# A two-layer hybrid decoder step on one core: all low weight halves of the first projection on GpSimd, four pairs of past rows to a weight block, small copies on ScalarE

## The reference, cut to what matters

```python
def even_project(x, w_in):
    h = jnp.einsum('btd,de->bte', x, w_in)
    a_val, a_glu, a_gate, q, kv_c, kv_s, kv_w, g, b_gate = jnp.split(h, offsets, axis=-1)
    u = a_val * jax.nn.sigmoid(a_glu)
    ...

def conv_branch(u_ext, a_gate, conv_w, conv_b, ln_g, ln_b):
    y = lax.conv_general_dilated(u_ext, conv_w[:, None, :], (1,), 'VALID', ...,
                                 feature_group_count=W_CONV) + conv_b
    return jax.nn.silu(layer_norm(y, ln_g, ln_b)) * jax.nn.silu(a_gate)

def compress_kv(kv, w_cmp):                # kv: 2048 past rows of a sequence, 256 wide
    ch = kv[:, :n_ch * CMP_STRIDE].reshape(B, n_ch, CMP_STRIDE, 2, KV_HEADS, HEAD_DIM)
    kc = (jnp.einsum('bnjchd,jchd->bnchd', ch[:, :-1], w_cmp[:CMP_STRIDE])
          + jnp.einsum('bnjchd,jchd->bnchd', ch[:, 1:], w_cmp[CMP_STRIDE:]))
```

## Time and profile before

| | us |
|---|---|
| median of 3 runs | 1334.58 (1334.31 to 1342.15) |
| the profiled execution, device time | 1331.57 |
| its span, first to last instruction | 1329.7 |
| PE busy | 1182.9 (89%) |
| DVE busy | 732.0 (55%) |
| POOL busy | 392.4 (30%) |
| ACT busy | 376.1 (28%) |

### The profile page before, as it was taken

How to read it: one execution, slowest core, us unless ns; L and a number is a source line. 1 busy time by engine, 2 the same in 40 slices (tenths; PEclk the granted TensorE clock), 3 DMA queues, 4 the chain that set the end, 5 groups by cost and what they waited for, 6 DMA issues and landing times.

```text
span 1329.7 us, 17791 instructions
## 1 busy us (share of the span) xinstructions
PE 1182.9 (89%) x7119; PEld 953.6 (72%) x7119; DVE 732.0 (55%) x1394; ACT 376.1 (28%) x791; POOL 392.4 (30%) x352
## 2 busy tenths in 40 slices
PE   5998999979989488899988999799969999978996
PEld 5998999979967244454544545478769999977883
DVE  2566889999934576445454454543435650065332
ACT  2211111111134454544545444511101121143000
POOL 3422200000012653432433323354412222124444
PEclk9998999989989588899999999899979999988998
DMA  7534333112130700040120301432112111041221
GB/s 225 184 108 154 112 96 80 32 32 48 32 157 0 263 11 1 1 159 1 45 114 1 159 1 69 129 106 93 52 52 79 47 47 39 9 145 52 95 95 40
DMA packets 77912, 105.22 MB, mean 79 GB/s; under 512 B 21280, under 2 KB 63912, under 8 KB 76607
## 3 DMA queue, kind: packets, MB, share of 16 engines
q1 hardware_dynamic: 69743, 69.62, 16.8%
q0 software_dynamic: 6016, 33.56, 6.8%
q10 hardware_dynamic: 2080, 1.05, 0.3%
HBM read 91.47 MB, written 17.69 MB: 82 GB/s over the span
## 4 chain that ended last, share of the span: by engine, by line
PE 63%; DVE 23%; ACT 5%; issue 4%; DMA 2%; POOL 1%; SPq 1%; POOLq 0%; ACTq 0%; DVEq 0%
PE PS L1511 15%; PE PS L1648 14%; DVE Y L543 9%; PE PS L648 9%; PE PS L1069 6%; PE PS L950 5%; PE PS L1083 3%; PE PS L640 2%; DVE ACC L495 2%; PE PS L1044 2%; PE PS L1003 2%; DVE WL L272 1%; PE PS L998 1%; ACT PRW L1109 1%; DVE PS L1163 1%
## 5 line engine op out<-in xcount | busy, mean ns | idle before, releaser
L648 PE MATMUL PS<-XH,WH 128*128 128x352 f32 (+1 forms) x648 | 149.2, 335 | 14.4 <-DVE WL L272 10.9
L543 DVE SCALAR_TENSOR_TENSOR Y<-U,SM,Y 128x1024 f32<-128x1024 f32 x120 | 145.9, 1279 | 0.2
L648 PE MATMUL PS<-XL,WH 128*128 128x352 f32 (+1 forms) x648 | 144.2, 327 | 0.0
L648 PE MATMUL PS<-XH,WL 128*128 128x352 f32 (+1 forms) x648 | 144.2, 327 | 0.0
L648 PEld LDWEIGHTS PS<-XH,WH 128*128 128x128 f32 (+1 forms) x648 | 110.0, 190 | 18.1 <-DVE WL L272 12.1
L648 PEld LDWEIGHTS PS<-XL,WH 128*128 128x128 f32 (+1 forms) x648 | 111.3, 189 | 1.4
L648 PEld LDWEIGHTS PS<-XH,WL 128*128 128x128 f32 (+1 forms) x648 | 111.0, 189 | 1.4
L1511 PE MATMUL PS<-WOH,XH 128*128 128x512 f32 (+1 forms) x288 | 94.2, 409 | 13.7 <-POOL WOL L1482 7.3
L495 DVE SCALAR_TENSOR_TENSOR ACC<-PS,SM,ACC 128x508 f32<-128x508 f32 x124 | 84.0, 740 | 40.5 <-PE PS L640 39.1
L950 PE MATMUL PS<-PT,TM 128*64 128x256 f32 x528 | 91.0, 425 | 12.4 <-ACT PT L1100 7.7
L1069 PE MATMUL PS<-KV,Q 64*128 64x512 f32 (+3 forms) x384 | 88.1, 515 | 15.2 <-ACT PRS L1109 12.4
(11 more groups left out here) (289 smaller groups left out, 2122.6 us busy)
## 6 DMA issues: line engine op xcount, KB each, us to landing
WRAW<-in_w_in_even SPq DMA_DIRECT2D x16, 512.0 KB, 4.3
WRAW<-in_w_in_odd SPq DMA_DIRECT2D x16, 512.0 KB, 3.9
XIN<-in_x_prompt SPq DMA_DIRECT2D x8, 512.0 KB, 12.5
WRAW<-in_w_in_even SPq DMA_DIRECT2D x16, 256.0 KB, 3.5
TM<-in_state_win_kv SPq DMA_DIRECT2D x8, 512.0 KB, 7.8
XR<-in_x_prompt SPq DMA_DIRECT2D x8, 512.0 KB, 3.5
layer_out<-R SPq DMA_DIRECT2D x8, 512.0 KB, 2.6
XR<-layer_out SPq DMA_DIRECT2D x8, 512.0 KB, 3.2
```

Source lines behind the costliest of these rows:

```text
L543: ins = v.scalar_tensor_tensor(dst, src, CWT[:, i, t:t + 1], dst, ALU.mult, ALU.add)
L648: ins = pe.matmul(PS[0:mcols, 3 * slot + c, 0:CH], w[:, slot, kk, 0:mcols], x[:, kk, c * CH:(c + 1) * CH], start=(kk == 0 and n == 0), sto ...
```

## The change

GpSimd makes all low halves, 0 to 26. Its program is now: low half m, then (for m below 8) gather m. Four pairs of past rows go with each of blocks 1 to 8, at `kk` = 0, 2, 4, 6. VectorE no longer makes low halves. Its order is: for each of blocks 1 to 8 four pairs, with `glu` behind the first pair of the even ones, and from block 5 on two taps or one behind the fourth pair; then 18 taps, `compress_prompt`, 6 taps, `conv_samples`, and the 94 taps that are left, in one go. The three small copies move to ScalarE, behind the evacuations of blocks 18 and 21.

```diff
-LOW_DVE = (6, 25)
 NPAIR = 32
+PER_BLOCK = 4
@@ pool_program @@
             low(po, 0)
             po.wait_ge(s_xt, 12)
             gather(0)
-            low(po, 1)
-            gather(1)
-            low(po, 2)
-            gather(2)
-            low(po, 3)
-            gather(3)
-            low(po, 4)
-            gather(4)
-            low(po, 5)
-            for n in range(5, 8):
-                gather(n)
-            for m in range(LOW_DVE[1], NM + 1):
-                po.wait_ge(s_wl, m)
+            for m in range(1, NM + 1):
                 low(po, m)
+                if m < 8:
+                    gather(m)
@@ act_program @@
                 evac(m)
                 if m + 2 <= NM:
                     high(m + 2)
+                if m == 18:
+                    act.wait_ge(s_ut, 1)
+                    act.activation(UROW[0:CW - 1, 0, :], PS[0:CW - 1, 6, :], ACT.Copy).then_inc(s_ue, 1)
+                    act.activation(UROW[:, 1, :], PS[0:NSAMP, 7, :], ACT.Copy).then_inc(s_ue, 1)
+                if m == 21:
+                    act.wait_ge(s_vct, 1)
+                    act.activation(VC[0:NCP, :], PS[0:NCP, 6, 0:P], ACT.Copy).then_inc(s_vc, 1)
@@ dve_program @@
-            def low_next(m):
-                if LOW_DVE[0] <= m < LOW_DVE[1]:
-                    v.wait_ge(s_wl, m)
-                    low(v, m)
-
-
-            for m in range(LOW_DVE[1]):
-                if m in (2, 4, 6, 8):
-                    glu(m // 2 - 1)
-                mine = range(min(3 * m - 3, NPAIR), min(3 * m, NPAIR)) if m else range(0)
-                few = 0 if m < 5 else (1 if m in (6, 8) else 2)
-                for n, p in enumerate(mine):
-                    compress(p)
-                    if m >= 5 and n < 2:
-                        taps(few if n else 1)
-                    if n == 1:
-                        low_next(m + 1)
-                if m and not mine:
-                    taps(3)
-                    low_next(m + 1)
-                    if m == 14:
-                        compress_prompt()
-                    elif m == 15:
-                        conv_samples()
-                        taps(3)
-                    else:
-                        taps(7)
-                if m == 19:
-                    v.wait_ge(s_ut, 1)
-                    v.tensor_copy(UROW[0:CW - 1, 0, :], PS[0:CW - 1, 6, :]).then_inc(s_ue, 1)
-                    v.tensor_copy(UROW[:, 1, :], PS[0:NSAMP, 7, :]).then_inc(s_ue, 1)
-                if m == 21:
-                    v.wait_ge(s_vct, 1)
-                    v.tensor_copy(VC[0:NCP, :], PS[0:NCP, 6, 0:P]).then_inc(s_vc, 1)
+
+            for m in range(1, 9):
+                for n in range(PER_BLOCK):
+                    compress(PER_BLOCK * (m - 1) + n)
+                    if n == 0 and m % 2 == 0:
+                        glu(m // 2 - 1)
+                if m >= 5:
+                    taps(2 if m % 2 else 1)
+            taps(18)
+            compress_prompt()
+            taps(6)
+            conv_samples()
             taps(len(TAPS))
@@ pe_program, one(m) @@
                 for kk in range(KT):
-                    if kk % 3 == 0 and 3 * (m - 1) + kk // 3 < NPAIR:
-                        compress(3 * (m - 1) + kk // 3)
+                    if kk % 2 == 0 and PER_BLOCK * (m - 1) + kk // 2 < NPAIR:
+                        compress(PER_BLOCK * (m - 1) + kk // 2)
                     ins = block(m, kk)
                 ins.then_inc(s_mm, 1)
```

## The result

| | before | after |
|---|---|---|
| median | 1334.44 us (4 runs, 1329.34 to 1342.15) | 1371.89 us (4 runs, 1360.68 to 1381.93) |
| ratio | | 1.025, 95% interval 1.016 to 1.033 |
| profiled execution, its span | 1331.57, 1329.7 | 1371.25, 1369.5 |
| end of block 8 | 166.3 | 172.4 |
| first mean | 371.1 | 403.5 |

The account below looks back on a forecast made before the run. TensorE, kept waiting by low halves that VectorE's taps lock out, bounds the first stage: 172.6 + 280.3 + 0.2 puts the first mean at 453.1, 82 us later. On 1331.6 that is 1413.6, plus 3.0 for the median: 1417, range 1330 to 1430.

Parts of the forecast that it names:

- the part with the pairs: Blocks 1 to 8, four pairs each: block 8 ends at 172.6 us, where it ended at 166.3.
- The turn of 3.93 us: From one pair's transposes to the next in blocks 1 to 8: 3.93 us, VectorE's, against 3.8 for TensorE alone.
- what glu and taps add: In blocks 1 to 8, VectorE's glu and taps between pairs make later pairs late, together 5 us.
- what is left without the collision: Rival "no cost": low halves run beside taps, TensorE bounds the first stage at 346.6, 24.3 less, 1310 us; chance 0.10.
- what a turn costs: Rival "a turn each": low halves enter at the next tap's end, VectorE pays 2.2 to 2.4; 1334 to 1338; chance 0.24.
- from one case to the other: The range: 1330, just below "a turn each" (0.24), to 1430, the upper end of "locked out" (0.58).
- I go by the earlier trace: Step taking a low half of 4.87 us, kept out until its taps ended, as the rule: "locked out", chance 0.58.
- three long waits: TensorE stands for low halves 10, 15 and 16, kept out by runs of taps: 14, 22 and 61 us.
- the two terms behind it: VectorE idle 9.6 us before `compress_prompt`, waiting for the store; lower TensorE clock after the long waits, 9 us.
- the two groups of rows: Earlier profile: a low half kept out by taps (4.87 us); a GpSimd subtraction let in between two VectorE ones (3.44).
- now and then: Rival: GpSimd wins some boundaries among the taps, so TensorE stands less; 1340 to 1410 us; chance 0.08.
- the yardstick: Start of the first mean, 371.1 before, forecast 453.1; its 82 us shift was carried to the kernel's end.

## Why the prediction was right and wrong

**Right: the part with the pairs.** Block 8 ended at 172.38, worked out as 172.6 (130.1 behind the first transposes, worked out as 130.9). The turn of 3.93 us held, and so did what glu and taps add.

**Right: what is left without the collision.** With a GpSimd that only writes the first mean starts at 345.7, worked out as 346.8; with the low halves on VectorE the sum for 354 was met at 354.8.

**Right: that GpSimd and VectorE exclude each other, and what a turn costs.** I had 2.2 to 2.4 us for a tap that gives way; measured 3.42 - 1.28 = 2.14. That the change came out slower is no luck either: the wait of 54.5 is one of the long waits forecast. That the time lies between 1330 and 1430 says little, since that range spans from one case to the other.

**Wrong: the step "I go by the earlier trace rows".** I took one low half that lost two boundaries for the rule, and made a sum of three long waits out of it: 14, 22 and 61 us for blocks 10, 15 and 16. Measured was one wait of 54.5, for block 20, and over three traces 7 losses in 23. The seven did what I had said of all (they waited until the run broke, the taps beside them at 1.20), but two thirds got in at once, as in the earlier trace rows. And a loser matters by where it falls: that of 197.50 lost two boundaries and cost TensorE nothing, since it was done in 5.12 and the slack was 7; early in the last run of 60 taps it costs what is left of the run. With it went the two terms behind it: low half 11 was never late, so the store of `ACC` didn't hold up `compress_prompt` (the 9.6 us of idleness; it began at 199.15, right behind the taps), and the lower clock was paid once (2.9 us), not three times. A sum with both behaviours, say some of the low halves losing and the last run of taps as the costly place, was what the two groups of rows allowed; I had it as a case of 0.08, "now and then", and gave it 1340 to 1410. The change lies in it.

**Too coarse: the yardstick.** I carried the shift of the first mean to the end one to one. Here 2.9 us came back behind it, because TensorE no longer stood in front of the means, and 10.7 came on in an attention that ran at another granted clock (415.8 to 430.4 us over the traces, whatever the version). A single pair of profiled executions can't be read to better than that.

The Trainium skill (SBUF — State Buffer, Who interferes with whom) has both engines' reads of this kind exclude each other, and a GpSimd instruction that only writes left in peace. The traces agree with both: 3.42 for the tap that gives way, 0.96 for every memset. Its rule that the order of issue decides describes the low halves that got in, 16 of 23 without breaks and all 52 with a break every 16 taps or fewer and another tap behind. It doesn't describe the 9 that let up to 51 later-issued taps go first, nor that of block 14, which in seven of eight traces let 2 to 8 short multiplications go first.

**Open:** what makes a low half lose its first boundary. It isn't the block (11, 12, 17, 19, 20, 21, 23 lost), nor the moment within the tap (among the taps, where VectorE didn't stand still, winners were issued 0.03 to 1.19 us ahead of the next instruction, losers 0.25 to 1.12; two more came 0.01 us ahead of a tap, let that one go and got in behind it). The number of taps since the last break or held-up tap goes with it: no loss up to the seventh, nothing but losses from the ninth on. It doesn't decide alone: 23 of 28 got in during an eighth tap, and ahead of the short multiplications a low half lost in the sixth. No run varied that number alone, and why it should count isn't shown. That a break every 16 taps did away with losses among taps (0 of 26, where 7 in 23 would give eight) goes with it in part: 16 of the 26 were issued in a seventh tap or earlier.

## What to carry to other kernels

Before work is moved to GpSimd, look at what VectorE does at the time: an instruction with two SBUF inputs on each of them takes turns at best, and then VectorE pays for nearly all of GpSimd's duration (2.14 us of 2.40 here, more than the 1.14 from the start of the same subtraction on VectorE itself to the start of the next instruction). In a long unbroken run of such instructions GpSimd may be kept out to the end, so what TensorE waits for shouldn't hang on it; a wait for VectorE's own last result every 16 instructions was enough to bound that. When two traces of one collision disagree, the sum needs a share for each and a place where the bad one falls, not the choice of one.

## What the hardware showed that I had not expected

- Being kept out is all or nothing: 9 low halves that lost one boundary among taps lost all that followed (2 to 51), and began within 0.2 us of the run's end. Seven more did the same ahead of or among short multiplications (2 to 8).
- One wait of some 0.1 us in 16 taps changes the outcome among taps: 21 executions within 14 us, against 1323 to 1379 with a break every 32 and 1360 to 1389 without.
- A gap of 1.19 us in VectorE's turn with TensorE took a subtraction of 1.21 us without the next turn being late.
